# A fused attention, expert and retention network on one core: the even layer's weight columns, head steps and output rows in another order

## The reference, cut to what matters

```python
h = rms_norm_2(x, norm_g)
(nq, nkc, nvc, nks, nvs, nkw, nvw, ng, nz, mq, mk, mv, mz, eq, ez) = _split(h @ w_in, EVEN_SPLITS)
kc = nsa_compress(rot(nkc), pe_k, w1_k, w2_k)
vc = nsa_compress(heads(nvc), pe_v, w1_v, w2_v)
gates = jax.nn.sigmoid(ng + gate_b).reshape(Bsz, T, NSA_BRANCHES, NSA_HEADS)
a_out = nsa_attention(rot(nq), kc, vc, rot(nks), heads(nvs), rot(nkw), heads(nvw), gates)
b_out = moba_attention(rot(mq), rot(mk), heads(mv))
m_out = memory_attention(heads(eq), mem_n, w_mem_kv)
y = jnp.concatenate([a_out * jax.nn.silu(nz), b_out * jax.nn.silu(mz),
                     m_out * jax.nn.silu(ez)], axis=-1) @ w_out
return x + y
```

## Time and profile before

| | |
|---|---|
| median of 3 runs | 2617.08 us (2608.99 to 2619.92) |
| the profiled execution | 2623.44 us, its span 2621.6 us |
| mean granted clock of TensorE | 0.954 |
| PE busy | 2485.2 us, 95% of the span |
| DVE, ACT busy | 1678.2 us, 1345.7 us |

### The profile page before, as it was taken

How to read it: one execution, slowest core, us unless ns; L and a number is a source line. 1 busy time by engine, 2 the same in 40 slices (tenths; PEclk the granted TensorE clock), 3 DMA queues, 4 the chain that set the end, 5 groups by cost and what they waited for, 6 DMA issues and landing times.

```text
span 2621.6 us, 44439 instructions
## 1 busy us (share of the span) xinstructions
PE 2485.2 (95%) x15412; PEld 2229.1 (85%) x15412; DVE 1678.2 (64%) x2990; ACT 1345.7 (51%) x2514; POOL 34.0 (1%) x79
## 2 busy tenths in 40 slices
PE   7999999999999999999999999999999799988988
PEld 7779999999988888889999999988888787777766
DVE  4444999677755555665998677655565547546454
ACT  3434555667655555444444776655554435634533
POOL 1000000000000000000000000000000000000000
PEclk9769999999999999999999999999999879779999
DMA  7215555444466666455555444566656523225443
GB/s 238 88 49 162 169 169 176 137 129 129 139 193 195 192 194 193 142 170 164 178 168 167 131 128 130 157 193 193 211 178 194 160 87 90 62 83 161 143 128 113
DMA packets 136421, 398.45 MB, mean 152 GB/s; under 512 B 12288, under 2 KB 13520, under 8 KB 135648
## 3 DMA queue, kind: packets, MB, share of 16 engines
q1 hardware_dynamic: 134144, 384.97, 47.7%
q0 software_dynamic: 2144, 11.71, 1.5%
HBM read 395.59 MB, written 1.05 MB: 151 GB/s over the span
## 4 chain that ended last, share of the span: by engine, by line
PE 69%; DVE 20%; ACT 5%; issue 4%; POOL 1%; DMA 1%; DVEq 0%; ACTq 0%; POOLq 0%; SPq 0%
PE bank L825 26%; PE bank L729 12%; PE bank L809 11%; PE bank L735 7%; DVE wl L1360 7%; PE bank L837 3%; PE bank L763 2%; PE bank L775 2%; ACT first L1172 2%; ACT wh L1059 1%; DVE arena L1527 1%; DVE arena L1528 1%; DVE arena L1530 1%; PE bank L768 1%; DVE arena L1529 1%
## 5 line engine op out<-in xcount | busy, mean ns | idle before, releaser
L1360 DVE TENSOR_TENSOR wl<-raw,wh 128x1024 fp32r<-128x1024 f32 (+1 forms) x732 | 893.6, 1223 | 661.4 <-ACT wh L1059 646.2
L1059 ACT ACTIVATE wh<-raw 128x1024 fp32r<-128x1024 f32 (+1 forms) x732 | 770.9, 1054 | 668.5 <-PE bank L825 342.0
L809 PE MATMUL bank<-xh,wh 128*128 128x256 f32 x2048 | 513.3, 288 | 5.3 <-issue 3.4
L809 PE MATMUL bank<-xl,wh 128*128 128x256 f32 x2048 | 502.4, 283 | 0.0
L809 PEld LDWEIGHTS bank<-xh,wh 128*128 128x128 f32 x2048 | 392.6, 192 | 7.3 <-DVE pairs L1598 3.8
L809 PEld LDWEIGHTS bank<-xl,wh 128*128 128x128 f32 x2048 | 393.2, 192 | 0.0
L809 PE MATMUL bank<-xh,wl 128*128 128x256 f32 x2048 | 293.1, 286 | 6.9 <-DVE wl L1360 6.8
L825 PE MATMUL bank<-wh,gl 128*128 128x512 f32 x1024 | 274.2, 389 | 1.6 <-DVE gl L1637 1.6
L825 PE MATMUL bank<-wh,gh 128*128 128x512 f32 x1024 | 274.1, 389 | 0.5 <-ACT gh L1189 0.5
L809 PEld LDWEIGHTS bank<-xh,wl 128*128 128x128 f32 x2048 | 262.9, 191 | 13.2 <-DVE wl L1360 11.5
L825 PE MATMUL bank<-wl,gh 128*128 128x512 f32 x1024 | 273.7, 389 | 0.0
(11 more groups left out here) (245 smaller groups left out, 2861.7 us busy)
## 6 DMA issues: line engine op xcount, KB each, us to landing
raw<-in_w_upT SPq DMA_DIRECT2D x256, 512.0 KB, 3.5
raw<-in_w_down SPq DMA_DIRECT2D x256, 512.0 KB, 3.5
raw<-in_l_w_in SPq DMA_DIRECT2D x84, 512.0 KB, 3.5
raw<-in_peer_w_query SPq DMA_DIRECT2D x32, 512.0 KB, 4.0
raw<-in_l_w_out SPq DMA_DIRECT2D x28, 512.0 KB, 3.8
raw<-in_attn_w_qkv SPq DMA_DIRECT2D x24, 512.0 KB, 3.8
raw<-in_conv_w_in SPq DMA_DIRECT2D x24, 512.0 KB, 3.9
arena<-in_na_bias POOLq DMA_DIRECT2D x1, 4096.0 KB, 12.3
```

The costliest lines, as they stand in the source:

```text
L809: last = pe.matmul(banks[b][:, 0:SEQ], lhsT=w[part][:, k, :], rhs=x_in[xp][:, k, :], start=(k == 0 and part == 0 and xp == 0), stop=(k == ...
L1059: act.activation(wh[:, n % SPLIT, 0:kts * cols], raw[:, n % RAW, 0:kts * cols], ACT.Copy)\
L1360: tt(wl[:, n % SPLIT, 0:kts * cols], raw[:, n % RAW, 0:kts * cols], wh[:, n % SPLIT, 0:kts * cols].bitcast(F32), ALU.subtract).then_inc(lo ...
```

## The change

It reorders the even layer and what stands around it.

- The column chunks are cut at other places and come in the order in which the heads' operands are wanted: (nkc nvc nks nvs), nq, (nkw nvw ng: the 280 columns), mq, mk, mv, (eq ez), nz, mz.
- Head steps start behind U12 instead of U16. The first 17 stand one to a unit; the other 14 stand two to a unit in U29 to U35, the first of the two between the unit's high and low products, the other behind it.
- The hidden product is cut in 8 pieces, two behind each of U7, U8, U9 and U10.
- Gates come last: silu of ez behind U27, nz behind U31, mz behind U35. The block heads' outputs go to a tile of their own (`moba_o`) and are multiplied with the gate at the end.
- The transposes of y are steps of the plan, two behind U34 and three after U35, and the output projection takes its rows in the order 0, 1, 4, 2, 3.
- Angles and sine move ahead of the norm of the layer, and the three loads of frequencies and masks further ahead in GpSimd's queue.

```diff
-E_YT = E_T
+E_YT = E_ROPED
+E_CMP = E_NSA + 1024
...
-EVEN_ROPES = (("nq", 0), ("nq", 1), ("nkc", 0), ("nkc", 1), ("nks", 0), ("nks", 1), ("nkw", 0), ("nkw", 1),
+EVEN_ROPES = (("nkc", 0), ("nkc", 1), ("nks", 0), ("nks", 1), ("nq", 0), ("nq", 1), ("nkw", 0), ("nkw", 1),
               ("mq", 0), ("mq", 1), ("mk", 0), ("mk", 1))
 ODD_CHUNKS = (0, 1, 2, 3, 12, 4, 5, 6, 7, 8, 9, 10, 11)
+EVEN_COLS = ((EVEN["nkc"], 512), (EVEN["nq"], 512), (EVEN["nkw"], EVEN["nz"] - EVEN["nkw"]), (EVEN["mq"], 512),
+             (EVEN["mk"], 512), (EVEN["mv"], 512), (EVEN["eq"], 512), (EVEN["nz"], 512), (EVEN["mz"], 512))
+EVEN_HEADS_AT, EVEN_SINGLE = 12, 17
 EVEN_PLAN = {
-    (0, 3): [("rope", 0)], (1, 0): [("rope", 1)], (1, 2): [("even_T", 0), ("even_T", 1)],
-    (1, 3): [("rope", 2), ("rope", 3)], (2, 0): [("rope", 4), ("rope", 5)],
-    (2, 1): [("even_T", 2), ("cmp_blocks", 0)], (2, 3): [("rope", 6), ("rope", 7), ("hid", 0), ("gates", 0)],
-    (3, 0): [("hid", 1), ("cmp_hidden", 0)], (3, 1): [("even_T", 3), ("even_T", 4)], (3, 2): [("kvc", 0), ("kvc", 1)],
-    (3, 3): [("cmp_S", 0), ("cmp_S", 1), ("cmp_softmax", 0)], (4, 1): [("cmp_T", 0)], (4, 2): [("cmp_O", 0), ("cmp_O", 1)],
-    (4, 3): [("rope", 8)], (5, 0): [("rope", 9)], (5, 2): [("even_T", 5), ("even_T", 6)],
-    (5, 3): [("rope", 10)], (6, 0): [("rope", 11)], (6, 2): [("even_T", 7), ("even_T", 8)],
-    (7, 3): [("silu", 0), ("silu", 1)], (8, 3): [("silu", 2), ("even_T", 9)],
+    (0, 3): [("rope", 0), ("rope", 1)], (1, 0): [("rope", 2), ("rope", 3), ("even_T", 0), ("cmp_blocks", 0)],
+    (1, 2): [("even_T", 1), ("hid", 0), ("hid", 1)], (1, 3): [("rope", 4), ("hid", 2), ("hid", 3)],
+    (2, 0): [("rope", 5), ("hid", 4), ("hid", 5)], (2, 1): [("hid", 6), ("hid", 7)],
+    (2, 2): [("cmp_hidden", 0), ("even_T", 2), ("even_T", 3)],
+    (2, 3): [("kvc", 0), ("kvc", 1), ("rope", 6), ("gates", 0)],
+    (3, 0): [("cmp_S", 0), ("cmp_S", 1), ("cmp_softmax", 0), ("rope", 7)], (3, 1): [("even_T", 4)],
+    (3, 2): [("cmp_T", 0), ("cmp_O", 0), ("cmp_O", 1)], (3, 3): [("rope", 8)], (4, 0): [("rope", 9)],
+    (4, 2): [("even_T", 5), ("even_T", 6)], (4, 3): [("rope", 10)], (5, 0): [("rope", 11)],
+    (5, 2): [("even_T", 7), ("even_T", 8)], (6, 3): [("silu", 2)], (7, 0): [("even_T", 9)], (7, 3): [("silu", 0)],
+    (8, 1): [("nsa_y", 0)], (8, 2): [("yT", 0), ("yT", 1), ("y_low", 0), ("y_low", 1)], (8, 3): [("silu", 1), ("mem_y", 0)],
+    (9, 0): [("yT", 2), ("y_low", 2), ("moba_y", 0), ("yT", 3), ("y_low", 3), ("yT", 4), ("y_low", 4)],
 }
+EVEN_YT = (0, 1, 4, 2, 3)
...
-EVEN_T_TILES = (0, 1, 7, 8, 9, 2, 3, 4, 5, 6)
-EVEN_ROPED = (2, 2, 4, 6, 8, 10, 10, 12, 12, 0)
-
-
-EVEN_CHUNKS = tuple(range(-(-EVEN_W // CHUNK)))
+EVEN_T_TILES = (7, 8, 0, 1, 9, 2, 3, 4, 5, 6)
+EVEN_ROPED = (2, 4, 6, 6, 8, 10, 10, 12, 12, 0)
+
+
 for _s in range(NSA_HEADS * 2 + MOBA_HEADS + MEM_HEADS + LAG["O"]):
-    _c = 4 + _s // 4
-    EVEN_PLAN.setdefault((_c, _s % 4) if _c < len(EVEN_CHUNKS) else (len(EVEN_CHUNKS), 0), []).append(("ev", _s))
+    _u = EVEN_HEADS_AT + _s if _s < EVEN_SINGLE else EVEN_HEADS_AT + EVEN_SINGLE + (_s - EVEN_SINGLE) // 2
+    _steps = EVEN_PLAN.setdefault((_u // 4, _u % 4), [])
+    _steps.insert(sum(kind == "ev" for kind, _ in _steps), ("ev", _s))
...
-        def weight(name, w, cols, order=None):
+        def weight(name, w, cols, order=None, chunks=None, rows=None):
 
             first_unit[name], chunk_end[name] = len(units), []
-            for c in order or range(-(-cols // CHUNK)):
-                c0 = c * CHUNK
-                n = min(CHUNK, cols - c0)
-                for k0 in range(0, w.shape[0], UKT * P):
+            for c0, n in chunks or [(c * CHUNK, min(CHUNK, cols - c * CHUNK)) for c in order or range(-(-cols // CHUNK))]:
+                for k0 in (g * UKT * P for g in rows or range(w.shape[0] // (UKT * P))):
...
-        weight("even_in", d["l0_w_in_2"], EVEN_W)
-        weight("even_out", d["l0_w_out_2"], D)
+        weight("even_in", d["l0_w_in_2"], EVEN_W, chunks=EVEN_COLS)
+        weight("even_out", d["l0_w_out_2"], D, rows=EVEN_YT)
...
+                        elif kind == "yT":
+                            J.add("even_yT", ring="other")
+                        elif kind in ("even_T", "kvc", "cmp_S", "cmp_T", "cmp_O", "odd_T", "ret_S") or kind == "hid" and k % 4 == 0:
                             J.add(kind, ring="other")
 
...
-        cmp_s = view(E_TMP, TT, NSA_HEADS, 32)
+        cmp_s = view(E_CMP, TT, NSA_HEADS, 32)
         vbd = view(E_APE, NSA_GROUPS, 4, HEAD)
-        cmp_pT = view(E_TMP + 512, TT, NSA_GROUPS, P)
+        cmp_pT = view(E_CMP + 512, TT, NSA_GROUPS, P)
         nsa_o = view(E_NSA, TT, 512)
+        moba_o = view(E_W1K, TT, 512)
...
+                    pool.dma_start(inv_freq, d["c_inv_freq"].partition_broadcast(P)).then_inc(extra_loaded["masks"], 16)
+                    pool.dma_start(causal, d["c_causal"]).then_inc(extra_loaded["masks"], 16)
+                    pool.dma_start(cmp_mask, d["c_cmp_mask"]).then_inc(extra_loaded["masks"], 16)
                     row_scales()
                 row_scales()
                 dump(("peer0", "peer1")[layer])
-            pool.dma_start(inv_freq, d["c_inv_freq"].partition_broadcast(P)).then_inc(extra_loaded["masks"], 16)
-            pool.dma_start(causal, d["c_causal"]).then_inc(extra_loaded["masks"], 16)
-            pool.dma_start(cmp_mask, d["c_cmp_mask"]).then_inc(extra_loaded["masks"], 16)
...
+                            if part == 0 and between:
+                                between(k0 // UKT)
...
+            def even_between(c, u):
+
+                steps = EVEN_PLAN.get((c, u), ())
+                if sum(kind == "ev" for kind, _ in steps) == 2:
+                    even_head(steps[0][1])
+
             def even_steps(c, u):
 
-                for kind, k in EVEN_PLAN.get((c, u), ()):
+                steps = EVEN_PLAN.get((c, u), ())
+                for kind, k in steps[sum(kind == "ev" for kind, _ in steps) == 2:]:
...
-                        j, r = take("hid", k), k * HEAD
+                        j, r = take("hid", k // 4) if k % 4 == 0 else J.of("hid", k // 4), k // 4 * HEAD
                         if k == 0:
                             pe.wait_ge(extra_loaded["cmpw"], 64)
                             pe.wait_ge(cmp_ready, 1)
-                        for i, kv in enumerate("kv"):
-                            for l in range(CMP_LEN):
-                                last = pe.matmul(bank(j)[r:r + HEAD, i * 16:i * 16 + N_CMP],
-                                                 lhsT=w1[kv][r:r + HEAD, l, :], rhs=ape[kv][r:r + HEAD, l, :],
-                                                 start=(l == 0), stop=(l == CMP_LEN - 1))
-                        done(last, j)
+                        i, kv = k // 2 % 2, "kv"[k // 2 % 2]
+                        for l in range(k % 2 * CMP_LEN // 2, (k % 2 + 1) * CMP_LEN // 2):
+                            last = pe.matmul(bank(j)[r:r + HEAD, i * 16:i * 16 + N_CMP],
+                                             lhsT=w1[kv][r:r + HEAD, l, :], rhs=ape[kv][r:r + HEAD, l, :],
+                                             start=(l == 0), stop=(l == CMP_LEN - 1))
+                        if k % 4 == 3:
+                            done(last, j)
...
+                        even_head(k)
+                    elif kind == "yT":
+                        j, g = take("even_yT", k), EVEN_YT[k]
+                        pe.wait_ge(y_ready, (1, 1, 2, 3, 4)[k])
+                        for q, src in enumerate(ev_y_src[i][:, t, :] for i in (2 * g, 2 * g + 1) for t in range(TT)):
+                            last = pe.transpose(bank(j)[:, q * P:(q + 1) * P], src, ident[:])
+                        done(last, j)
+
+            def even_head(k):
+
+                for g in {0: (1, 2, 3), 8: (4,), 16: (5, 6, 7, 8), 24: (9,)}.get(k, ()):
+                    wait_read(pe, J.of("even_T", g))
+                if k == 16 + LAG["O"]:
+                    for t in range(TT):
+                        wait_read(pe, J.of("even_in", 2 * 5 + t))
+                attention("ev", EV, ev_heads, head_base["ev"], head_step(EV, k))
...
+            act.wait_ge(angle_ready, 1)
+            act.activation(view(ROPE_AT, 2 * TT * ROPES), view(ROPE_AT, 2 * TT * ROPES), ACT.Sin).then_inc(tables, 1)
+            act.wait_ge(tables, 1)
...
-            act.wait_ge(angle_ready, 1)
-            act.activation(view(ROPE_AT, 2 * TT * ROPES), view(ROPE_AT, 2 * TT * ROPES), ACT.Sin).then_inc(tables, 1)
-            act.wait_ge(tables, 1)
...
-            split_x("even_yT", ev_out, count_=5)
...
+                    elif kind == "yT":
+                        split_x("even_yT", ev_out, some=[k])
...
-            norm_rows(1)
-            lows(first_unit["mem1"], 0)
-            norm_scale("even")
-            lows(unit_of[J.of("mem1", 0)], 0)
-            norm_parts("even", "even_in")
...
+            lows(first_unit["mem1"], 0)
...
+            norm_rows(1)
```

(38 more changed lines are left out.)

60 lines of the change are left out of this document (24 added, 36 removed).

## The result

The changed kernel's median is 2630.35 us (2625.29 to 2637.27, 10 runs), beside 2619.11 of the kernel before on the same chip (10 runs): ratio 1.0043, interval 1.0027 to 1.0059. It is slower by 0.4%, within half a per cent; the forecast was 2603.8, and its range ended at 2627. The profiled execution took 2633.73 us, 10.3 more than that of before.

What follows compares the result with a forecast made beforehand. PE was taken as nearly always busy, its clock deciding: even-layer terms summed to 245.8 us with the clock up, plus 10 and 6 for the lower clock, 261.8 against 275.1. Taken off the median: 2603.8 us, range 2584 to 2627.

Steps and rivals of the forecast that it cites:

- The double units, +6 for the clock: U29 to U35, two head steps each: 56.5 us with the clock up, plus 6 for time at the lower clock.
- period of 8.0: Each double unit takes 8.0 us, because the second step's output matmul waits for ACT's copy behind the high part.
- The hidden product, +10 for the clock: Hidden product with U7 to U11: 24.6 us at the upper clock, plus 10 taken between nothing and 21.
- two idles: PE's waits of 2.4 and 2.0 us ahead of the hidden product, a reason given for its clock loss.
- isn't helped: Rival: hidden product and its units stay at the lower clock, +11 over the sum, 2615 us, no change; chance 0.23.
- summed wait of 2.4 for the key ropes: After U4 PE waits 2.4 us before the transposes of kc; a second wait, before the hidden product, is 2.0.
- its 8.8: From the end of U35 to the output projection: 8.8 us for last output, silu, products, transposes and splits.
- the sine: Start of the even layer: moving angles and sine removes 7.6 us of idle and slow unit, net -3.4 us.
- mem1 4.2 later: Start of the even projection: mem1's first matmul comes 4.2 us later, behind the moved angle and sine work.
- single units at 70.6: Fourteen units with one head step each, U15 to U28, take 70.6 us.
- the softmax's two waits: PE waits 5.4 us ahead of the transposes of kw and 2.4 ahead of the compressed output.
- the slower rival: Rival: all double units run at the lower clock because steps outweigh dense products, 12.7 us each, 2631 us; chance 0.15.

Runs made afterwards that it cites:

- x2: Changed kernel with ScalarE doing a double unit's first-step exponentials and copy ahead of the high part: 2610.7 us, ratio 0.9953 to the kernel before.
- x9: x8 with the hidden product's pairs behind U11 to U14, among 512-column units, and heads starting at U17: 2594.8 us, ratio 0.9908 to the kernel before.
- x5: Changed kernel with the hidden product cut to 16 of its 256 matmul records, waits and copies kept: 2604.9 us, ratio 0.9932 to the kernel before.
- x3: Changed kernel with one head step per unit to the end and seven steps behind U35: 2615.0 us, ratio 0.9974 to the kernel before.
- x6: x2 with the transposes of kw and the compressed output moved behind U15: 2605.8 us, ratio 0.9940 to the kernel before.
- x7: x2 with the silus of ez and nz together in one slot, behind U31: 2606.9 us, ratio 0.9941 to the kernel before.
- x8: x2 with the edits of x6 and x7 together: 2602.3 us, ratio 0.9927 to the kernel before.
- x12: x8 with the edits of x9 and x11 together: 2596.5 us, ratio 0.9909 to the kernel before.
- x11: x8 with the first three groups of y transposes all behind U35, ahead of the wait for DVE: 2595.9 us, ratio 0.9912 to the kernel before.
- x1: Kernel before with only the angles and sine moved ahead of the layer's norm, and the three mask loads with them: 2617.3 us, ratio 0.999.

## Why the prediction was wrong

*The double units, +6 for the clock: mis-sized. They took 17.9 us more than their 56.5 in the sum.* The prediction named the wait (ACT's copy behind the high part) and its period of 8.0, and the first unit shows it, 8.5 from wait to wait. The step that failed is the one behind: it took the clock from the mix of steps and dense products, "nearer" 1.00. x2 keeps the mix and takes the wait: clock 1.00 over four units, and 56.2 us from U29 to the end of U35 against 74.4. PE is busy 62.2 us there in the changed kernel and 53.4 in x2, of which 14.0 at a clock of 0.51, so some 46 would be left at the upper clock throughout (an estimate from these windows). By that some 16 of the 17.9 are the clock, where 6 was taken, and some 2 are waits. The wait in every unit had to be priced with the lower clock that follows it. The cure was in the prediction's own sentence, an order on ACT.

*The hidden product, +10 for the clock: mis-sized, 17.2 of a bound of 21.* Of the 7.2 over the 10, 1.3 are the upper price (3.90 a piece in x9, 3.6 summed); the rest is clock. The prediction weighed "two idles" and a share of PE's work. x5 kept the idles and, without the product, lost the fall but for U7: it is the product that holds the clock down. What has to stand between its pieces to bring the clock up stays open. For the width of the units speaks that U7, 512 columns, brought the second piece partly up and the 280-column units brought the third and fourth not at all, here and in x2, x3, x6, x7 and x8, and that x9 and x12, with 512-column units between, nearly lost the fall. Against it speak two pieces right behind a 280-column unit, x9's first (4.28) and x11's third (4.21). The rival "isn't helped" was the nearer one (21 by it, 17.2 measured), and its reason, that one dense unit brought back 2 us, was the row to go by.

*Smaller ones.* Up to the first hidden product 2.0: U0 took 4.2 us instead of 2.75, and U5, behind the summed wait of 2.4 for the key ropes, 4.4, both partly at the lower clock; against that the second wait was 0.59 where 2.0 was summed. The end 1.5: the prediction gives its 8.8 without items; the twelve y transposes in it ran at the lower clock (1.94 us for eight; x2 has eight in 1.04 behind U34), by an estimate from these 1.3 of it. The output projection 1.4: its first unit is wholly at the lower clock, in the earlier trace rows partly. That the reordered rows hide only the last splits no run tests; by x11 the split of the transposes hides nothing.

*Right by size:* the sine (net -3.4 said; the distance fell 6.1 in x1, its whole time 0 to 5), mem1 4.2 later (4.1), single units at 70.6 (70.9), and the softmax's two waits (7.8 said, 7.1). x6 shows that a later slot covers the first of these two.

The time came out at the slower rival's, 2631, but only half by it: its place holds 11.9 (17.9 less the 6 taken) of the 24.7 us between forecast and measurement in the profiled execution, and its condition, steps outweighing dense products, was not the cause.

## What to carry to other kernels

When a change fills PE's gaps with small work, price each wait that stays inside the dense stretch twice, with itself and with the lower clock behind it, and look first at the order of the engine that it waits for: one exchange on ACT turned 0.4% slower into 0.5% faster. For small products look for a row at either clock before pricing them: the same 256 records took 24.5 us in the changed kernel, 16.3 and 15.9 where they stood among 512-column units (x9, x12), and what made the difference is not separated. And a term whose bounds are 0 and 21 needs a row that tells which end, or the range must hold both.

## What was not expected of the hardware

The same code ran its hidden product in 20.7 to 24.6 us in two executions (x11, x8), and in the first the wait ahead of it was 0.60 instead of 2.12. The changed kernel had a wait of 0.59 there and 24.5 us all the same, so the wait alone doesn't tell; what does is open. A wait of 1.54 us on PE left the clock where it was the first time (2250.60) and had it at the lower level the second (2259.14), 8.5 us later. One wait behind U32 was followed by some 14 us at the lower clock in x2 (wait 1.96) and by some 4 in x7 (2.48), so how long the fall lasts isn't told by the wait's length. The 32 records of the compressed scores took 3.29 us in the changed kernel and 5.4 in x8, one execution each.
